# Two attention heads per product with values, and no ring banks for gates: a change to a two-layer hybrid transformer block

## The reference, cut to what matters

```python
def block(args):
    qx, kx, vx, mx = args
    s_loc = jnp.einsum('bqhgd,bkhd->bhgqk', qx, kx).astype(F32) * scale
    s_loc = jnp.where(mx[None, None, None], s_loc, NEG_INF)
    s_ctx = jnp.einsum('bqhgd,bchd->bhgqc', qx, kc).astype(F32) * scale
    p = jax.nn.softmax(jnp.concatenate([s_loc, s_ctx, sink_col], axis=-1), axis=-1).astype(vx.dtype)
    return (jnp.einsum('bhgqk,bkhd->bqhgd', p[..., :span], vx)
            + jnp.einsum('bhgqc,bchd->bqhgd', p[..., span:span + L], vc))
```

## Time and profile before

| | us |
|---|---|
| median of 3 runs | 2886.79 (2883.69 to 2890.5) |
| the profiled execution | 2884.82 |
| its span, first to last instruction | 2883.0 |
| TensorE busy in the span | 2785.7 (97%) |
| VectorE, ScalarE, GpSimd busy | 1280.2, 1010.8, 1112.2 |

### The profile page before, as it was taken

How to read it: one execution, slowest core, us unless ns; L and a number is a source line. 1 busy time by engine, 2 the same in 40 slices (tenths; PEclk the granted TensorE clock), 3 DMA queues, 4 the chain that set the end, 5 groups by cost and what they waited for, 6 DMA issues and landing times. The chain is left out here.

```text
span 2883.0 us, 43950 instructions
## 1 busy us (share of the span) xinstructions
PE 2785.7 (97%) x17300; PEld 2430.5 (84%) x17300; DVE 1280.2 (44%) x2843; ACT 1010.8 (35%) x1864; POOL 1112.2 (39%) x976
## 2 busy tenths in 40 slices
PE   7999899999999999999999989999999999899998
PEld 5888788999998897888888878877989888888887
DVE  4654537524453035333333555644725441344446
ACT  4333236533332225222222253324633332433332
POOL 2333221153333333333433344333154435465555
PEclk9999999999999999999999999999999999999999
DMA  5111210022223133212112331122032322522223
GB/s 237 59 59 67 81 66 23 16 92 88 89 74 118 59 150 114 73 59 73 59 59 73 110 125 53 58 95 81 9 106 74 106 71 88 205 88 102 88 101 112
DMA packets 39370, 249.54 MB, mean 87 GB/s; under 512 B 4480, under 2 KB 4864, under 8 KB 13568
## 3 DMA queue, kind: packets, MB, share of 16 engines
q1 hardware_dynamic: 36288, 236.25, 23.1%
q10 hardware_dynamic: 2880, 10.49, 0.9%
HBM read 236.23 MB, written 10.49 MB: 86 GB/s over the span
## 5 line engine op out<-in xcount | busy, mean ns | idle before, releaser
L2334 POOL TENSOR_TENSOR w_rest<-raw,w_head 128x512 fp32r<-128x512 f32 (+1 forms) x634 | 830.7, 1343 | 934.0 <-ACT w_head L1376 915.4
L945 PE MATMUL psum_products<-h_head,w_head 128*128 128x512 f32 (+2 forms) x2288 | 823.2, 360 | 4.3 <-POOL w_rest L2342 1.5
L945 PE MATMUL psum_products<-h_head,w_rest 128*128 128x512 f32 (+2 forms) x2288 | 804.2, 351 | 0.0
L945 PE MATMUL psum_products<-h_rest,w_head 128*128 128x512 f32 (+2 forms) x2288 | 804.1, 351 | 0.0
L945 PEld LDWEIGHTS psum_products<-h_head,w_head 128*128 128x128 f32 (+1 forms) x2288 | 430.1, 188 | 65.1 <-DVE h_rest L1813 2.4
L945 PEld LDWEIGHTS psum_products<-h_rest,w_head 128*128 128x128 f32 (+1 forms) x2288 | 429.5, 188 | 64.3
L945 PEld LDWEIGHTS psum_products<-h_head,w_rest 128*128 128x128 f32 (+1 forms) x2288 | 430.5, 188 | 56.1 <-issue 1.0
L1376 ACT ACTIVATE w_head<-raw 128x1024 fp32r<-128x1024 f32 (+1 forms) x321 | 320.7, 1045 | 402.8 <-PE psum_products L945 344.9
L945 PE MATMUL psum_products<-w_head,h_head 128*128 128x256 f32 x1408 | 402.3, 286 | 1.6 <-DVE h_rest L1873 1.6
L945 PE MATMUL psum_products<-w_rest,h_head 128*128 128x256 f32 x1408 | 390.6, 277 | 0.0
L945 PE MATMUL psum_products<-w_head,h_rest 128*128 128x256 f32 x1408 | 390.4, 277 | 0.0
(11 more groups left out here) (278 smaller groups left out, 3787.7 us busy)
## 6 DMA issues: line engine op xcount, KB each, us to landing
raw<-in_stream SPq DMA_DIRECT2D x184, 1024.0 KB, 4.9
raw<-in_stream SPq DMA_DIRECT2D x16, 512.0 KB, 3.5
mods_mid<-in_stream SPq DMA_DIRECT2D x8, 1024.0 KB, 10.4
residual<-stage ACTq DMA_DIRECT2D x16, 512.0 KB, 2.6
stage<-residual SPq DMA_DIRECT2D x14, 512.0 KB, 5.2
mods_b<-in_stream SPq DMA_DIRECT2D x5, 1024.0 KB, 24.5
mods_a<-in_stream SPq DMA_DIRECT2D x3, 1024.0 KB, 13.6
x_in<-in_x SPq DMA_DIRECT2D x4, 512.0 KB, 8.4
```

The lines of the kernel that those rows point to most:

```text
L945: return nc.tensor.matmul(o, a, b, start=start, stop=stop)
L2334: G.tensor_tensor(wl[:, s["sp"] % 2, a:b], place_of(s)[:, a:b], wh[:, s["sp"] % 2, a:b].bitcast(F32), ALU.subtract).then_inc(*ev.mark("poo ...
```

## The change

The heads of a tile are taken in pairs (g, g+4), one from each key/value head. Every second tick multiplies a pair with the values: the values are stationary, 64 columns per head, one head in each 64-column half of the array, and 128 columns of probabilities stream. The output is already turned. The reciprocals of the two heads are spread over 64 rows each by a product with the identity, copied to SBUF by ScalarE (`arc`) and multiplied in by VectorE, once a pair. The four closing transposes and their copy go. The turned probabilities get a third buffer. Fill comes only behind odd ticks, and values are multiplied in even ones.

`rows` and `columns` in the MLP of layer 0 use mixer bank 4 and are spread over u=1 to 3 (before: 1 and 2). The second `gates` becomes `gates_late`, which uses mixer banks 0 to 3 and stands ahead of `rows`. In layer 1 two of the four rests after the mixers are made one step earlier.

```diff
-    def ticks(kind, count, fill=iter(()), pieces=0, start=0, stop=None, banks=lambda i: 0, **k):
+    def ticks(kind, count, fill=iter(()), pieces=0, start=0, stop=None, banks=lambda i: 0, every=1, **k):
...
-            upto = round((i + 1) * pieces / count)
+            upto = round((i + 1) // every * pieces / (count // every))
...
-        heads = [(t, hd) for t in tiles for hd in range(AH)]
-        ticks("attend", AH * len(tiles) + 4, fill, 12 * len(pairs(ctx)) - 6, l=l,
-              heads=heads, banks=lambda i: int(tile_ends(heads, i)))
+        heads = [(t, g + 4 * half) for t in tiles for g in range(4) for half in range(2)]
+        ticks("attend", AH * len(tiles) + 4, fill, 12 * len(pairs(ctx)) - 6, l=l, heads=heads, every=2)
...
-                    if ctx and k == 4:
-                        split_more(s, (1,), (0, 1))
+                    if k == len(tiles) - 2:
+                        split_more(s, (1,) if ctx else (), (0, 1))
...
-        split_more(s, (), (2, 3) if ctx else range(4))
+        split_more(s, (), (2, 3))
...
-                more = vectors(2) if ctx else iter(())
+                more = vectors(2, mixer=True) if ctx else iter(())
+            if u == 1:
+                step("gates_late", l=l, which=1, ctx=ctx)
             if u:
-                for _ in islice(more, 1 if u == 1 else 3):
+                for _ in islice(more, (0, 1, 2, 1)[u] if u < 4 else 0):
                     pass
-            if u == 1:
-                step("gates", None, 4, l=l, which=1, ctx=ctx)
...
+        def rows_bank(st):
+
+            return psm[:, 4, :] if st["mixer"] else psg[:, st["bank"] % RING, :]
...
+                        pair = (i_ - 4) // 2 if i_ >= 4 and i_ % 2 == 0 else None
...
-                            pe.wait_ge(*ev.at("apt", l, j))
-                            if j >= 1:
-                                pe.wait_ge(*ev.at("ay", l, j - 1))
+                        if pair is not None:
+                            t, _ = st["heads"][2 * pair]
+                            pe.wait_ge(*ev.at("apt", l, 2 * pair + 1))
+                            if pair >= 1:
+                                pe.wait_ge(*ev.at("ay", l, pair - 1))
                             keys = akeys(t)
                             for m, kt_ in enumerate(keys):
-                                last = mm(psm[:, 4, 0:AD], apt[:, j % 2, m * P:(m + 1) * P],
-                                          av[:, kt_, lo:lo + AD], m == 0, m == len(keys) - 1)
-                            last.then_inc(*ev.mark("pe", "apv", l, j))
-                        if tile_ends(st["heads"], i_):
...
-                            for m in range(4):
-                                last = nc.tensor.transpose(psg[:, st["bank"] % RING, m * P:(m + 1) * P],
-                                                           ay[:, t % 2, m * P:(m + 1) * P], c("ident"))
+                                for half in range(2):
+                                    lo = half * AD
+                                    last = mm(psm[lo:lo + AD, 4, 0:P], av[:, kt_, lo:lo + AD],
+                                              apt[:, (2 * pair + half) % 3, m * P:(m + 1) * P],
+                                              m == 0, m == len(keys) - 1)
+                            last.then_inc(*ev.mark("pe", "apv", l, pair))
+                            pe.wait_ge(*ev.at("ard", l, 2 * pair + 1))
+                            for half in range(2):
+                                lo, s0 = half * AD, 64 + 8 * ((2 * pair + half) % 4)
+                                last = mm(psm[lo:lo + AD, 4, P:2 * P],
+                                          small[:, s0 + 5:s0 + 6].broadcast_to((P, AD)), c("ident"))
+                            last.then_inc(*ev.mark("pe", "arT", l, pair))
...
+                        if i_ >= 5 and i_ % 2:
+
+                            pair = (i_ - 5) // 2
+                            act.wait_ge(*ev.at("arT", l, pair))
+                            if pair >= 1:
+                                act.wait_ge(*ev.at("ay", l, pair - 1))
+                            nc.scalar.activation(arc[:], psm[:, 4, P:2 * P], ACT.Copy).then_inc(
+                                *ev.mark("act", "arc", l, pair))
...
-                            V.tensor_scalar(ay[:, t % 2, hd * AD:(hd + 1) * AD], psm[:, 4, 0:AD],
-                                            small[:, s0 + 5:s0 + 6], None, ALU.mult).then_inc(
-                                *ev.mark("dve", "ay", l, j))
+                        if i_ >= 5 and i_ % 2:
+                            pair = (i_ - 5) // 2
+                            t, hd = st["heads"][2 * pair]
+                            dve.wait_ge(*ev.at("apv", l, pair))
+                            dve.wait_ge(*ev.at("arc", l, pair))
+
+                            V.tensor_tensor(ya[:, t, hd, :], psm[:, 4, 0:P], arc[:], ALU.mult).then_inc(
+                                *ev.mark("dve", "ay", l, pair))
```

More of the change, by code:

```diff
@@ L110, in param_places @@
     return place, n
-def tile_ends(heads, i):
-    return i >= 4 and heads[i - 4][1] == AH - 1
 def make_plan():
@@ L173, in columns, with vectors @@
         if rows["quarter"] == 3:
-            st = step("columns", l=rows["l"], v=rows["v"], g=rows["g"])
+            st = step("columns", l=rows["l"], v=rows["v"], g=rows["g"], mixer=rows["mixer"])
             st["bank"] = rows["bank"]
-    def vectors(count, homes=False):
+    def vectors(count, homes=False, mixer=False):
         due, mids = None, []
@@ L185, in vectors @@
             made[0] += part == 0
-            now = step("rows", s, 1, l=l, v=v, g=made[0] - 1, quarter=part)
+            now = step("rows", s, 0 if mixer else 1, l=l, v=v, g=made[0] - 1, quarter=part, mixer=mixer)
             yield
@@ L1065, in _ @@
                     pe.wait_ge(*ev.at("silu_c"))
-                    free_bank(st["bank"])
+                    if not st["mixer"]:
+                        free_bank(st["bank"])
+                    elif st["quarter"]:
+                        pe.wait_ge(*ev.at("rows_sb", l, st["v"], st["quarter"] - 1))
                     w = raw_of(s)
-                    bank = psg[:, st["bank"] % RING, :]
+                    bank = rows_bank(st)
                     for k in range(2):
@@ L1077, in _ @@
                     for ct in range(2):
-                        last = nc.tensor.transpose(psg[:, st["bank"] % RING, ct * P:(ct + 1) * P],
+                        last = nc.tensor.transpose(rows_bank(st)[:, ct * P:(ct + 1) * P],
                                                    vrow[:, st["g"] % 2, ct * P:(ct + 1) * P], c("ident"))
-                    last.then_inc(*ev.mark("pe", "bank", st["bank"]))
+                    last.then_inc(*(ev.mark("pe", "turned") if st["mixer"] else ev.mark("pe", "bank", st["bank"])))
                     ev.now[("vturn", st["g"])] = {"pe": ev.count["pe"]}
+                elif kind == "gates_late":
+                    pe.wait_ge(*ev.at("vec", l, 23))
+                    for n, q, half in gate_banks(dict(bank=0, ctx=st["ctx"])):
+                        for j in range(4):
+                            m = 5 * KD + 4 * half + j
+                            last = nc.tensor.transpose(psm[:, n, j * P:(j + 1) * P],
+                                                       vec[:, l, m, q:q + 1].broadcast_to((P, P)), c("ident"))
+                        last.then_inc(*ev.mark("pe", "gates_late", l, n))
                 elif kind == "gates":
@@ L1609, in _ @@
                                                      *ev.mark("act", "ap", l, i_))
-                        if tile_ends(st["heads"], i_):
-                            t = st["heads"][i_ - 4][0]
-                            act.wait_ge(*ev.at("bank", st["bank"]))
-                            nc.scalar.activation(yT_of("a", 4, t),
-                                                 psg[:, st["bank"] % RING, :].rearrange("p (k c) -> p k c", k=4),
-                                                 ACT.Copy).then_inc(*ev.mark("act", "bank_free", st["bank"]))
-                            ev.now[("yT", l, "a", t)] = {"act": ev.count["act"]}
                 elif kind == "rqk_sb":
@@ L1781, in _ @@
                     n, m = st["bank"], st["v"] * KD
-                    dve.wait_ge(*ev.at("bank", n))
-                    src = psg[:, n % RING, 0:COLS].rearrange("p (b a r) -> p a b r", b=2, a=4)[:, :, :, 0:2]
+                    dve.wait_ge(*(ev.at("vturn", st["g"]) if st["mixer"] else ev.at("bank", n)))
+                    src = rows_bank(st)[:, 0:COLS].rearrange("p (b a r) -> p a b r", b=2, a=4)[:, :, :, 0:2]
                     bias = pr(l, "mod_b", m, KD).rearrange("p (a b r) -> p a b r", a=4, b=2).broadcast_to((P, 4, 2, 2))
                     V.tensor_tensor(vec[:, l, m:m + KD, :].rearrange("p (a b) r -> p a b r", a=4), src, bias,
-                                    ALU.add).then_inc(*ev.mark("dve", "bank_free", n))
+                                    ALU.add).then_inc(
```

(7 more changed lines are left out.)

50 lines of the change are left out of this document (18 added, 32 removed).

## The result

The changed kernel takes 2854.53 us (median of 4 runs, 2853.18 to 2855.95), the kernel before 2885.95 beside it (4 runs, 2883.69 to 2890.5): a ratio of 0.9889, interval 0.9874 to 0.9905, some 31 us less. Forecast were 2862 and a range of 2852 to 2881. The profiled execution took 2854.76 us, its span 2853.0, which is 30.0 less than that of before.

What follows compares the result with a forecast made beforehand. TensorE's own occupation, 97% of the span, was taken as the bound. Values 19.8, ScalarE -3, layer 0's MLP 6.9 and layer 1's rests 1.5 sum to 25.2 us less, so 2862 us; range 2852 to 2881.

Steps and rivals of the forecast that it cites:

- Rounds and excursions: Attention: both halves run side by side at 0.11 us a round; entering and leaving them costs 0.32 us a pair.
- C: Attention: weight loads of the halves don't hide under the 0.11 us streams; 22 us, so 2884, no change; chance 0.12.
- The gain of the values: Attention: pairs gain 0.71, 0.47 or 0.11 us with five, four or two key tiles, 19.8 us in all.
- the 0.81 for four key tiles: Attention before the change: one head's values hold TensorE 0.81 us, plus 0.08 behind, 0.89 in all.
- ScalarE's lumps: Attention: two 1045 ns gate-weight copies in a row, three times per layer, cost 0.5 us each time; -3 us.
- The MLP's start: Layer 0's MLP: waits of gates (2.4 us) and columns (2.8 us) go; 6.9 us together, ends 2.4 and 6.9.
- Layer 1's rests: Layer 1's first MLP block: two rests made earlier remove TensorE's waits of 0.28 and 1.25 us for GpSimd; 1.5 us.
- The low end of -1: Layer 1's rests: the gain becomes -1 us if GpSimd, working in its former gap, slows VectorE's norms.
- A clock that falls elsewhere: Sign of a wrong prediction: the clock falls at places other than layer 0's MLP; no size given.
- B: Attention: half of the 0.55 us hand-over shows in each of 40 pairs, giving back 11 us; 2873; chance 0.16.
- D: Attention: the 64-column halves run one after the other, 0.11 us more for each of 400 rounds; 2906; chance 0.10.
- the sum with all high ends: Whole kernel: 19.8 + 6.9 + 2 = 28.7 us gained if every term reaches its high end.

Runs made afterwards that it cites:

- the fill in every tick: Changed kernel with the gate projections spread over all ticks again instead of only behind odd ones; 2867.37 us.
- the kernel with the attention alone: Changed kernel with the start of layer 0's MLP and the rests of layer 1's first MLP weights put back as before; 2864.63 us.
- the one with the gates in the ring: Changed kernel with layer 0's second gates back in ring banks, at their new place; 2861.95 us.
- the kernel with two excursions: Changed kernel with the reciprocals' product moved ahead of the probabilities' transposes, so each pair enters and leaves the halves twice; 2865.66 us.
- setting two copies apart: Changed kernel with ScalarE's two 1045 ns copies per gate weight two ticks apart in five of six attention places; 2854.06 us.
- the sink's column alone: Changed kernel with reciprocals turned by one transpose per pair, spread by a copy behind the exponential's minimum, and the sink's logit as a scores column; 2849.3 us.
- the last version: The kernel of the sink's column alone, with ScalarE's two 1045 ns copies also set apart by two ticks; 2847.38 us.

## Why the prediction was right, and where its sizes were off

**Rounds and excursions: right.** A pair with five key tiles costs 0.09 + 1.46 + 0.11 = 1.66 us (forecast 1.64), with four 1.44 (1.42), with two 1.01 (0.98). No load of 64 columns shows between rounds (C): rounds follow each other at 0.109, while each load is drawn 0.137 long beside the running products.

That the load of 128 columns sets the rate of the old way is the prediction's inference. The loads of the values with five key tiles, in the kernel before and in the changed one:

```profile
2045.69 1.20 PEld L945 LDWEIGHTS psum_mixers<-a_v,a_pt 128*128 128x128 f32 x10
```

```profile
507.25 1.07 PEld L942 LDWEIGHTS psum_mixers<-a_pt,a_v 128*64 128x64 f32 x20 [0.17 <-issue]
```

Without the drawn length of the last one, 0.19 and 0.14 us, loads of 128 columns start 0.11 us apart and those of 64 columns 0.05. That agrees with the inference; no run changed the width of the loads alone.

**The gain of the values: 19.8 forecast, 21.6 found** as TensorE's busy time (248.9 to 227.3 over both stretches). Two terms for the kernel before were too small. The first is "Two key tiles, at that rate, are 0.41 + 0.08 = 0.49"; no row had been read for them. The timeline of before, layer 0:

```profile
452.42 0.56 PE L945 MATMUL psum_mixers<-a_v,a_pt 128*128 128x64 f32 x4
452.79 0.36 PE L945 MATMUL psum_products<-h_head,w_head 128*128 128x256 f32 x1
...
454.68 0.56 PE L945 MATMUL psum_mixers<-a_v,a_pt 128*128 128x64 f32 x4
455.23 0.36 PE L945 MATMUL psum_mixers<-a_k_head,a_q_split 128*128 128x256 f32 x1
```

Ahead of fill the four passes hold TensorE 0.36 to 0.44 us, ahead of the next scores 0.55, and over the 16 heads 0.48 in the mean, without the idle time that the trace shows. With the 0.08 behind that is 0.56, 0.07 more than forecast. The second is the 0.81 for four key tiles, read from one head: over the 32 heads the mean is 0.855. With 16 x 0.07 and 32 x 0.045 the old way cost 1.1 + 1.4 = 2.5 us more. The new way costs 0.02 to 0.03 a pair more than forecast, 0.9 in all. That leaves 1.6 of the 1.8 us. Part of the longer holds of the old way may be waits so short that the drawn lengths cover them; this was not separated.

**What becomes late next: named rightly, netted wrongly.** The forecast was -3 us for ScalarE's lumps. The waits for a_pt did rise, from 1.2 to 3.3 us over both stretches, and stand right behind the two copies. But TensorE's waits for `ay`, 2.7 us in the kernel before, fell to 0.4, which the sum had left out. Before (layer 0, two rows, and layer 1), then the changed kernel (layer 0; none in layer 1):

```profile
PE psum_mixers L945 <- DVE a_y L2231: 1.2, 5, 0.4
PE psum_products L1310 <- DVE a_y L2231: 0.4, 1, 0.4
PE psum_mixers L945 <- DVE a_y L2231: 1.1, 2, 0.5
...
PE psum_mixers L942 <- DVE a_y_turned L2246: 0.4, 1, 0.4
```

A pair is now handed over once, with a whole piece of fill ahead of the next product; which of the two counts was not separated (with the fill in every tick these waits are 2.2 us again). All waits together went from 7.4 to 7.8. So the attention gained 21.3 where 16.8 stood: 1.8 from TensorE's busy time and 2.7 from this term.

**The MLP's start: 6.9 forecast, 7.2 found.** Both waits are gone (4.99 us idle to none) and the clock stands at 1.00 in the whole stretch. Of the 6.9 the two waits made up 2.4 and 2.8; the other 1.7 us stood for the fall of the clock, and no run shows that term by itself. What the runs show in its place is TensorE's busy time in the stretch, 67.65 before and 65.41 after, 2.2 us less, and the products behind the wait in the kernel before:

```profile
1168.18 0.42 PE L945 MATMUL psum_products<-h_head,w_rest 128*128 128x256 f32 x1
1168.40 0.42 PE L945 MATMUL psum_products<-h_rest,w_head 128*128 128x256 f32 x1
...
1171.50 0.28 PE L945 MATMUL psum_products<-h_rest,w_head 128*128 128x256 f32 x1
1171.62 0.28 PE L945 MATMUL psum_products<-h_head,w_head 128*128 128x256 f32 x1
```

```profile
1168.10:1171.30 3.20, 3.20 (x17) 3.20 (x16) 0.00 (x0) 2.00 (x2) 2.60 (x2) 0.50 0.88 364
```

At a granted clock of 0.50 they start 0.21 us apart, behind it 0.12. Sixteen of them, from 1167.97 to 1171.38, thus took some 1.5 us longer, an estimate from these starts. That there is one fall, behind the wait of `columns`, fits the kernel before and not the others: the kernel with the attention alone has the same two waits and two falls (a mean of 0.79 over the 8 us around each), and the one with the gates in the ring has a fall behind the gates' wait (0.79 as well).

**Layer 1's rests: 1.5 forecast, 1.1 found.** Both waits for GpSimd, 1.5 us, are gone, and TensorE's idle time fell by 2.0 us in all; but the granted clock, 1.00 before, is 0.93 in this stretch, and TensorE's busy time grew by 0.9. The low end of -1, for a GpSimd that slows VectorE, was the author's estimate: VectorE's 29 instructions there are busy for 18.49 us against 18.03, and what made the difference is not shown. A clock that falls elsewhere was named ahead as a sign of being wrong, and this is one, of less than a microsecond. Against the kernel with the attention alone, where the clock is 0.94 there, the stretch gains 2.2.

**Rivals.** B is out: 0.4 us of waits for the multiplication in 40 pairs. C and D are out by the timeline of a pair. No other engine took over: VectorE and ScalarE are busy for 71 and 70% of layer 0's attention stretch, and for 75 and 68% of layer 1's; between 490 and 530 us, where five key tiles stand, for 75 and 73% (forecast 77 and 79%).

**How much was luck.** The sum's 25.2 us became 30.0 in the traces, 4.5 of the difference in the attention. That is more than the sum with all high ends, 28.7, so 2854.5 lies in the stated range only by the 6 us that were added for the spread of the runs. Of the 7.1 us between 2861.6 and 2854.5 the sum accounts for 4.8. Most of the rest, 2.2, is chance: the median stood 2.0 above the profiled execution before, and 0.2 below it after.

## What to carry to other kernels

Where a pass of 64 columns past 128 stationary ones takes about as long as a pass of 128 columns (here 0.10 and 0.11 us), make the narrow operand stationary and put two of them into the halves: alternate them (in turn, a pair with five key tiles took 0.70 us longer), and count about 0.3 us of TensorE for each way into the halves and back (0.29 in the kernel with two excursions). When a tick gets shorter, list every wait that its partner engines cause *now*, and not only the ones that will appear; those that vanish count as much. Then look at which engine's lump stands in the tick: here setting two copies apart gained about 1 us by itself, relieving the engines and shortening TensorE's work 4.6 us in the attention stretches, and both together 7.1. And before a difference of 1 or 2 us between two traces is put down to an edit, compare the granted clock of the two stretches (in layer 1's attention 1.00 and 0.98 were 1.4 us apart with the same work).

## What was not expected of the hardware

With all of one half's passes first, the other half's passes start up to three or four passes early (with five key tiles at 509.57, from where two passes start in every 0.11 us up to 509.89), and a pair with two key tiles took the same time in both orders. Starts of different halves do not even follow the program: in the experiment with the halves in turn the first half's product for the reciprocals starts at 510.28, ahead of the second half's last values (510.38 and later), which stand before it in the program.

VectorE's reciprocal of 64 equal columns took 543 ns where one column took 153; the copy that spreads one column over 64 took 274 with the sink's column alone and 247 in the last version.

Identical dense stretches of 256-column products run at one of two rates. The same 320 matmuls at a granted clock of 1.00, in the kernel before and in the changed one:

```profile
1030.12:1066.16 36.04, 36.04 (x320) 36.04 (x319) 5.11 (x9) 4.03 (x4) 14.12 (x12) 1.00 0.61 238
```

```profile
1017.70:1055.15 37.45, 37.45 (x320) 37.45 (x319) 5.10 (x9) 4.02 (x4) 13.96 (x11) 1.00 0.59 228
```

That is 113 or 118 ns per pass, 1.4 us here, kept for tens of microseconds. In the other eleven profiles these matmuls take one of the same two times. Which of the two a stretch gets differs between kernels that do the same work there; what sets it was not tried.
